# Where the activations lie in SBUF against the weights' rings, in a two-block transformer kernel on one core

## The reference

```python
for l in range(2):                        # first block
    h = rms_norm(x, pre_mix_g[l])
    x = x + rms_norm(parallel_mixer(h, ...), post_mix_g[l])      # LRU, forgetting attention, retention
    h = rms_norm(x, pre_cross_g[l])
    x = x + rms_norm(memory_cross_attention(h, mem_n, ...), post_cross_g[l])
    h = rms_norm(x, pre_ffn_g[l])
    x = x + rms_norm(swiglu(h, w_gate[l], w_up[l], w_down[l]), post_ffn_g[l])
for l in range(2):                        # second block
    x = x + 0.5 * swiglu(rms_norm(x, ffn1_norm[l]), ...)
    h = rms_norm(x, mix_norm[l])          # NSA, stick-breaking and sliding-window attention
    x = x + merged_branches(h @ w_in[l]) @ w_out[l]
    x = x + 0.5 * swiglu(rms_norm(x, ffn2_norm[l]), ...)
```

## Time and profile before

| | |
|---|---|
| runs | 2411.73 us median of 3 (2409.66 to 2414.92) |
| profiled execution | 2410.42 us, of which the span from first to last instruction is 2409.1 |
| granted TensorE clock, mean | 0.956 of the full speed |
| TensorE busy with matmuls | 2204.7 us, 92% |
| VectorE, ScalarE, GpSimd busy | 1425.1, 1132.5, 94.7 us |
| from HBM | 356.61 MB read, 149 GB/s over the span |

### The profile page before, as it was taken

One profiled execution on the slowest core, in us unless ns is written; L12 is line 12 of the kernel. 1 busy time (PEld: TensorE's weight loads), 2 busy tenths in 40 slices (PEclk: granted clock), 3 DMA queues, 4 the chain that ended last, 5 costly groups with the idle time before them and its releaser, 6 DMA issues.

```text
span 2409.1 us, 40450 instructions
## 1 busy us (share of the span) xinstructions
PE 2204.7 (92%) x17158; PEld 2113.4 (88%) x17158; DVE 1425.1 (59%) x2190; ACT 1132.5 (47%) x1744; POOL 94.7 (4%) x95
## 2 busy tenths in 40 slices
PE   6987989979887799989998988999999988988999
PEld 6866889979777799989997877999999988878999
DVE  5655565555646565465566556655655674657654
ACT  4544444444544444444444556544444444465443
POOL 4100010000000000000000000000000000000000
PEclk9989999989899999989998999999999998989999
DMA  5423346635323255645544223555555542234554
GB/s 206 153 81 111 106 134 203 214 124 176 105 95 115 93 187 181 199 148 187 190 161 158 71 88 106 180 181 192 180 183 193 177 155 88 88 106 140 185 183 158
DMA packets 98484, 360.30 MB, mean 150 GB/s; under 512 B 11136, under 2 KB 11149, under 8 KB 97920
## 3 DMA queue, kind: packets, MB, share of 16 engines
q1 hardware_dynamic: 96192, 349.22, 44.5%
q0 software_dynamic: 1680, 5.35, 0.7%
q10 hardware_dynamic: 432, 3.15, 0.3%
HBM read 356.61 MB, written 3.43 MB: 149 GB/s over the span
## 4 chain that ended last, share of the span: by engine, by line
PE 75%; DVE 13%; ACT 7%; issue 3%; POOL 1%; DMA 0%; ACTq 0%; DVEq 0%; SPq 0%; POOLq 0%
PE bank L272 67%; DVE w_lo L1268 3%; ACT w_hi L783 2%; PE bank L326 1%; DVE xn_lo L1290 1%; PE bank L643 1%; DVE sq L1325 1%; PE bank L308 1%; POOL sq L1882 1%; PE bank L331 1%; DVE x L1329 1%; DVE sq L1838 1%; PE bank L327 1%; PE bank L616 1%; DMA raw<-in_stream 0%
## 5 line engine op out<-in xcount | busy, mean ns | idle before, releaser
L1268 DVE TENSOR_TENSOR w_lo<-raw,w_hi 128x1024 fp32r<-128x1024 f32 x664 | 806.9, 1251 | 422.1 <-ACT w_hi L783 421.9
L272 PE MATMUL bank<-xn_hi,w_hi 128*128 128x256 f32 x3168 | 915.7, 289 | 93.8 <-DVE xn_lo L1290 81.1
L272 PE MATMUL bank<-xn_lo,w_hi 128*128 128x256 f32 x3168 | 907.6, 286 | 0.0
L272 PE MATMUL bank<-xn_hi,w_lo 128*128 128x256 f32 x3168 | 906.9, 286 | 0.0
L783 ACT ACTIVATE w_hi<-raw 128x1024 fp32r<-128x1024 f32 x664 | 671.4, 1049 | 231.8 <-PE bank L272 228.8
L272 PEld LDWEIGHTS bank<-xn_hi,w_hi 128*128 128x128 f32 x3168 | 619.5, 196 | 106.7 <-issue 104.5
L272 PEld LDWEIGHTS bank<-xn_lo,w_hi 128*128 128x128 f32 x3168 | 619.7, 196 | 0.2
L272 PEld LDWEIGHTS bank<-xn_hi,w_lo 128*128 128x128 f32 x3168 | 619.1, 195 | 0.0
L272 PE MATMUL bank<-hid_lo,w_hi 128*128 128x256 f32 x1056 | 291.8, 276 | 0.0
L272 PE MATMUL bank<-hid_hi,w_hi 128*128 128x256 f32 x1056 | 291.8, 276 | 0.0
L272 PE MATMUL bank<-hid_hi,w_lo 128*128 128x256 f32 x1056 | 291.8, 276 | 0.0
(11 more groups left out here) (344 smaller groups left out, 2757.7 us busy)
## 6 DMA issues: line engine op xcount, KB each, us to landing
raw<-in_stream SPq DMA_DIRECT2D x664, 512.0 KB, 4.2
skew<-vec POOLq DMA_DIRECT2D x12, 192.0 KB, 3.9
table<-skew POOLq DMA_DIRECT2D x1, 1408.0 KB, 7.3
con<-in_con ACTq DMA_DIRECT2D x1, 1029.0 KB, 15.1
x<-in_x ACTq DMA_DIRECT2D x1, 1024.0 KB, 6.9
xn<-in_mem ACTq DMA_DIRECT2D x1, 1024.0 KB, 11.5
out<-x SPq DMA_DIRECT2D x4, 256.0 KB, 4.4
logit<-in_small POOLq DMA_DIRECT2D x3, 288.5 KB, 3.0
```

The lines of the kernel that those rows point to most:

```text
L272: m = T.matmul(out, a, b, start=first and j == 0, stop=True, skip_group_check=True)
L1268: V.tensor_tensor(w_lo[m % RING], raw[m % RING], w_hi[m % RING].bitcast(F32), ALU.subtract).then_inc(*lo_done.next())
```

## The change

The 64 bytes of slack behind `shared` are taken away. x, xn, xn_hi, xn_lo, y_hi and y_lo are allocated directly behind `shared`, then a tile of 64 bytes that nothing uses, then the three rings. sq and all that follows keep their addresses. The program of every engine is the same but for these addresses.

```diff
-    nc.alloc_sbuf_tensor("shared", [P, shared // 4 + 16], F32)
+    nc.alloc_sbuf_tensor("shared", [P, shared // 4], F32)
...
-    raw = [sb(f"raw{r}", [P, HK, COLS]) for r in range(RING)]
-    w_hi = [sb(f"w_hi{r}", [P, HK, COLS], F32R) for r in range(RING)]
-    w_lo = [sb(f"w_lo{r}", [P, HK, COLS], F32R) for r in range(RING)]
     x = sb("x", [P, KT, S])
     xn = sb("xn", [P, KT, S])
     xn_hi, xn_lo = sb("xn_hi", [P, KT, S], F32R), sb("xn_lo", [P, KT, S], F32R)
     y_hi, y_lo = sb("y_hi", [P, KT, S], F32R), sb("y_lo", [P, KT, S], F32R)
+
+    sb("offset", [P, 16])
+    raw = [sb(f"raw{r}", [P, HK, COLS]) for r in range(RING)]
+    w_hi = [sb(f"w_hi{r}", [P, HK, COLS], F32R) for r in range(RING)]
+    w_lo = [sb(f"w_lo{r}", [P, HK, COLS], F32R) for r in range(RING)]
     sq = sb("sq", [P, KT, S])
```

## The result

The changed kernel takes 2388.57 us (median of 4 runs, 2382.61 to 2396.97), the kernel before 2413.32 (median of 4, 2409.66 to 2421.09). The ratio is 0.9897, with a 95% interval of 0.9874 to 0.9921: about 25 us faster. The forecast was 2361.0, that is 50.6 us. The sign was right, the size was off by half; the result lies nearer to rival A (2393), whose condition, the slow one of the two steps nearly everywhere, turned out to hold in four of the six swiglus.

The account below looks back on a forecast made before the run. TensorE, busy for 92% of the span, was taken to bound the kernel; 46.0 + 4.6 = 50.6 us off the profiled 2410.4 gave 2359.8, and with 1.3 to the median 2361, range 2344 to 2394.

Parts of the forecast that it names:

- rival A: Products streaming xn and y: the slow steady step (118 ns) nearly everywhere, 18.3 us less, 2393 us; chance 0.12.
- Slow tiles stand at the same place in a row as the weights that are loaded meanwhile: Split matmuls: xn and y, placed like the loaded weights, step at 120 ns; tiles 64 bytes away at 113.3 or 118.
- Rival B: Products of xn and y: addresses are not the cause, something like their stage is; nothing changes, 2411.7 us; chance 0.10.
- Rival C: Distance at large counts, not place in a row: hid, mem, merged fall to 120, xn stays; 2438 us; chance 0.04.
- 120 by these stamps: Compressed blocks loaded, one ring tile streamed: three products behind nine at 113.3 ns take 120 each (0.36 us).
- I take three quarters at 113.3 and one at 118: Paying products of xn and y: 6,868 save 6.7 ns and 2,290 save 2.0 ns, 50.6 us together.
- 9,158 products: Products streaming xn and y taken to pay, out of 10,656, after leaving out those at half clock or hidden by waits.
- Products of hid, merged and mem: the same distance as before, so 0 us: Down stages and other streams of these tiles: no change expected; were the distance lost, 6.7 ns for each.
- No transfer came late: Ring halves must come every 2.72 us instead of 2.88, 193 GB/s; 211 GB/s was seen, so 0 us.
- The splits cost the same: Weight splits keep their places in a row, at 1.25 us each: 0 us; one per cent more would be 8 us.
- At half the clock: At 1.2 GHz, addresses do not set the step; 250 products, five slots behind the norms, were taken off.
- The mean clock: Idle stretches keep their length, so the mean clock should stay at 0.956; 5 us either way allowed.

Follow-up runs that it names:

- same_place: The changed kernel with the rings directly behind y_lo, so that everything lies at byte 128 of a row: 2437.51 us, ratio 1.0104.
- apart_192: The changed kernel with the rings 192 bytes behind the activations' place instead of 64: 2407.57 us in one run.
- behind_64: The kernel before with 64 bytes put between the rings and x, xn and y staying behind the rings: 2405.58 us, ratio 0.9975.
- kick_12: The changed kernel with twelve extra products, same ring tile loaded and streamed, before the first up slot of each of six FFNs: 2366.91 us, ratio 0.9818.
- kick_apart: The changed kernel with twelve extra products per FFN that stream xn_hi past the loaded ring tile, 64 bytes apart: 2400.61 us, ratio 0.9949.
- kick_all: The changed kernel with twelve extra same-tile products per FFN and also ahead of three more stages, twelve places in all: 2366.32 us, ratio 0.9815.
- before_pause: The kernel before, with TensorE waiting for ScalarE's root before the first up slot in each of six FFNs: 2413.02 us, ratio 0.9998.

## Why the prediction came out as it did

**The mechanism held.** "Slow tiles stand at the same place in a row as the weights that are loaded meanwhile": shown by same_place, where moving only the rings by 64 bytes puts all kinds at 120.0. Rival B is out, since xn and y changed with the addresses alone. Rival C is out: hid lost its step in part, but xn did not stay at 120, and with apart_192 and behind_64 distance at large made no 120 either. One support was weaker than it looked: the last three distances of the earlier trace rows, "120 by these stamps", are 351 ns in the unrounded starts, 117.0 each, so that the rows have no step of 120; it took same_place to show the pair. (And 119.7 and 113.0 ns from the earlier trace rows divide by all products that a window counts; less the two that don't start in it, they are 120.0 and 113.4.) By the Trainium skill (TensorE: Matmul & The Clock Gate, Step-by-step: what each phase is for), loading the next weights takes no read bandwidth of SBUF from the running matmul. The runs disagree as to the pace: with one set of shapes same_place is at 120.0 ns throughout, where the changed kernel is at 113.3 or 117.8. They don't show that the read ports are the reason.

**The first step that failed: "I take three quarters at 113.3 and one at 118".** Measured in the profiled execution, two of the six gate/up stages took 113.3 and four 117.8. The evidence behind the share was "all six hid stages run fast, which they enter straight from another product". The fact was right and the reading the wrong way round: they entered it from products at 120, and kick_12 against kick_apart shows that just this brings 113.3. For a stage that starts behind other work the rows had 113.3 twice (mem, and merged in one layer by its printed durations) and 118 twice (merged where the starts were read, and the ring past mem); that was the better guide. In the forecast the six gate/up stages had 6,048 of the 9,158 products, and so 33.4 of the 50.6 us. Measured, from the first product of each to the first of its down stage, the six take 779.4 us before and 759.2 after: 20.2, so 13.2 us of the miss.

**The second: "Products of hid, merged and mem: the same distance as before, so 0 us".** The distance was the same, but a run holds its step across a change of tile. hid now follows xn at 117.8 in four swiglus: 4 x 528 x 4.5 ns = 9.5 us lost (9.0 by the stages' lengths, 359.4 us before and 368.4 after). In the forecast no row stood for this, because before the change the products in front of hid were always at 120.

**The sum again, by the measured steps.** Gate/up of the swiglus: 2 x 1,008 x 6.7 = 13.5 and 4 x 1,008 x 2.2 = 8.9 us. y: 1,152 x 6.3 = 7.3. The other 1,958 products of xn that pay lie between 2.2 and 6.7 ns each, 4.3 to 13.1. Less hid's 9.5, that is 24.5 to 33.3 us. The half clock takes some 4 us back (below): 20 to 29, against 22.0 between the profiled spans and 25 between the medians. In kick_12 the six gate/up stages, extra products and all, take 745.6 us, 33.8 less than before, and hid 358.8, 0.6 less; the rest of the kernel gives the remaining 8.7 of the 43.1 between the spans.

**The other terms.** No transfer came late: within the fast stages the ring brought in 215 GB/s where the earlier trace rows had 206. The splits cost the same, as taken. At half the clock the places make no difference, as taken: the distances there are 213 or 214 ns, before, after and in same_place. The mean clock did not stay: it fell from 0.956 to 0.950. At a granted 0.50, 387 split products stood so far apart before and 432 after, so 45 more at some 97 ns each, 4 us; that is inside the 5 us either way that the forecast gave it, and a small part of the 28.6 missed.

**What stays open.** Why 64 bytes the other way (behind_64) and 192 bytes had 117.8 in every swiglu; how few products of the slow pair are enough, between 4 and 12; whether places repeat after 1 KB or sooner; and what in the chip makes the two places matter. All of it was seen on tiles of one shape.

## What to carry to other kernels

Read the distance between starts and not the printed duration, and compare it between stages of the same shape: one of 120 ns beside one of 113.3 pointed at the layout. Put the tile that is streamed and the one that is loaded 64 bytes apart in a row of 1 KB, and then check each stage, since the step it runs at can be that of the stage in front of it. A step that is fast "six times of six" at one entry says little about another: ask what ran just before in each.

## What the runs showed of the hardware

- One shape (128 x 128 loaded, 128 x 256 streamed, float32r, weights loaded for every product) at the full clock has three steady steps: 120.0 ns with both tiles at the same place of a 1 KB row (or 512 bytes from it, as half of the loaded tiles are), and 113.3 or 117.8 with 64 bytes between them. With 32 bytes it is 118.3, with 96 one of 117.3, 118.7 and 120.0.
- The choice between 113.3 and 117.8 is made at the start of a run of products, holds for over 1,500 products and over a change of the streamed tile, and can be made anew by a break, in either direction: in the rows shown, a start that comes 0.67 us (117.5 to 114) or 0.39 us (114 to 118.6) after the one before it.
- At a granted clock of 0.50 the same products stand 213 or 214 ns apart, in the kernel before, the changed one and same_place alike.
- A run at 64 bytes that follows directly on twelve or more products of the slow pair came to 113.3 in all six swiglus, in each of kick_12, kick_all, the kernel before and before_pause (there hid behind xn). Slower products in front made the next ones faster.
- Where the draw is left open the time spreads: 14 us over 4 runs of the changed kernel and 25 us over 10 of kick_apart, against 4 us over 4 runs of same_place and 8 over 4 of kick_12. That the draws differ between executions is a likely reason, not shown: only one execution of each was profiled, and the kernel before, with few products open to a draw, spreads by 9 to 15 us over 7 to 21 runs too.
